# Whole chunks instead of half chunks behind the two norms of a 256-token sequence

## The chip, the cores and the metric

One NeuronCore of a Trainium2 chip runs the whole program in one launch. The metric is device time in microseconds, from the first to the last instruction; lower is better. The program is a bidirectional encoder layer over two sequences, one of 256 tokens and one of 512.

## What is computed

The reference, cut to what matters here:

```python
def encoder_layer(x, ...):
    h = rmsnorm(x, norm1_g)
    proj = h @ w_in                                  # 1024 -> 3584 columns
    ...                                              # attention heads, retention heads
    x = x + jnp.concatenate([na_o, ret_o], axis=-1) @ w_out
    x = x + peer(rmsnorm(x, norm2_g), peer_w_q, peer_sub_keys, peer_u, peer_v)
    return x

def peer(h, w_q, sub_keys, u, v):
    q = (ht @ w_q)...                                # 1024 -> 2048 columns
    ...                                              # top keys, experts, gelu(h @ u), @ v
```

`reference()` applies this to `x_prompt` (256 tokens) and `x_sample` (512 tokens), then a last norm.

## The kernel before

All five engines run hand-written programs that are ordered by semaphores. The sequence index is `q`: 0 for the 256 tokens (`TILES[0] = 2` tiles of 128 tokens) and 1 for the 512 tokens (4 tiles). The order of stages is `front(0)`, 128 expert steps for `q = 0`, `front(1)`, 128 expert steps for `q = 1`, then the sum over expert rows and the last norm.

`front(q)` reads 52 weight chunks of 512 KB in a fixed order (`C_NA_QK` 0 to 7, `C_NA_V` 8 to 11, and so on, up to `C_WQ` 36 to 51). Each chunk goes through a ring of `RING = 4` slots: SyncE loads it to `raw` once the chunk four places ahead has been split, ScalarE copies it to the rounded high part `sp_hi` (line 536) when its slot has been read, and VectorE makes the low part `sp_lo = raw - sp_hi` (line 1145). The normalised tokens are held in the same way, as `ht_hi` and `ht_lo`. A product in full precision is then three matmuls: high by high, low by high, high by low. All these are matmuls of type fp32r.

Behind a norm, VectorE scales a token tile into `h_tile` (line 1170), TensorE turns it by 8 transposes (`turn`, line 845), ScalarE writes `ht_hi` out of PSUM (line 570), and VectorE writes `ht_lo` (`turned_lo`, line 1181, counted by the semaphore `lo_evac`). This is done tile by tile.

A channel-major chunk is 8 x 3 = 24 matmuls that add up in one PSUM bank. `t_part` (line 863) runs them over all tokens of the sequence: 256 columns for `q = 0`, 512 for `q = 1`. `t_half` (line 879) runs them over half of the tokens: 128 columns for `q = 0`, 256 for `q = 1`. `first_chunks` runs the first two chunks behind a norm in halves, so that the first halves can start when half of the tiles have been turned. It is called for chunks 0 and 1 of the 256-token sequence, for chunks `C_WQ` and `C_WQ + 1` of both sequences, and nowhere else. The chunks that follow are run whole. `front(0)` has 8 channel-major chunks behind the first norm, then token-major ones with 512 columns (line 833), and 16 behind the second norm, then `key_scores` (line 1052).

VectorE's program between the first norm and the fourth chunk holds `log_decays`, a chain of small operations; its `lo(0, 3)` stands after it.

Of the kernel before, what the change touches and what calls it, by code (L numbers as in the profile page):

```python
# [79 lines left out]
def encoder_program(nc, a):  # L80
# [3 lines left out]
    with ctx:  # L84
# [159 lines left out]
        def counted(q, name, n):  # L244

            return S[name], (first_counts[name] if q else 0) + n

        def tile_cols(t):
            return slice(t * P, (t + 1) * P)
# [4 lines left out]
        def slot_of(q, c):  # L254
            return c % RING
# [4 lines left out]
        def t_index(c):  # L260

            return c if c < C_NA_V else c - 4 if c < C_RET_V else c - 20
# [566 lines left out]
        def _(pe):  # L829
# [7 lines left out]
            def turn(q, n, i):  # L837

                tt = n * TILES[q] + i
                pe.wait_ge(*counted(q, "src_ready", tt + 1))  # L840
                if i >= 2:
                    pe.wait_ge(*counted(q, "lo_evac", tt - 1))
                bank = 2 + 2 * (tt % 2)
                for k in range(KD):
                    last = pe.transpose(ps[:, bank + k // 4, tile_cols(k % 4)], h_tile[:, i % 2, tile_cols(k)],
                                        s["ident"][:, :])
                last.then_inc(S["tr_done"], 1)

            def t_part(q, c, first, end):

                n, w = t_index(c), TILES[q] * P
                sl = slot_of(q, c)
                if first == 0:
                    pe.wait_ge(*counted(q, "lo_ready", c + 1))
                    if n >= 2:
                        pe.wait_ge(*counted(q, "t_evac", n - 1))
                    elif q:
                        pe.wait_ge(S["gelu_done"], N_KEYS - 1 + n)
                for e in range(first, end):
                    k, which = e // 3, e % 3  # L860
                    lhs = (sp_hi, sp_hi, sp_lo)[which][:, sl, k * P:(k + 1) * P]
                    x = (ht_hi, ht_lo, ht_hi)[which][q][:, k, :]
                    last = pe.matmul(ps[:, n % 2, 0:w], lhs, x, start=e == 0, stop=e == 23, skip_group_check=True)  # L863
                if end == 24:
                    last.then_inc(S["t_done"], 1)

            def t_half(q, c, m):

                n, w = t_index(c), TILES[q] * P // 2
                sl, cols = slot_of(q, c), slice(m * w, m * w + w)  # L870
                if m == 0:
                    pe.wait_ge(*counted(q, "lo_ready", c + 1))
                    if n >= 2:
                        pe.wait_ge(*counted(q, "t_evac", n - 1))
                for e in range(24):
                    k, which = e // 3, e % 3
                    lhs = (sp_hi, sp_hi, sp_lo)[which][:, sl, k * P:(k + 1) * P]
                    x = (ht_hi, ht_lo, ht_hi)[which][q][:, k, cols]
                    last = pe.matmul(ps[:, n % 2, cols], lhs, x, start=e == 0, stop=e == 23, skip_group_check=True)  # L879
                if m == 1:  # L880
                    last.then_inc(S["t_done"], 1)

            def first_chunks(q, n, c):

                nt = TILES[q]
                for i in range(nt - 1):
                    turn(q, n, i)
                if nt == 2:
                    turn(q, n, 1)
                pe.wait_ge(*counted(q, "lo_evac", n * nt + nt // 2))  # L890
                t_half(q, c, 0)
                if nt > 2:
                    turn(q, n, nt - 1)
                t_half(q, c + 1, 0)
                pe.wait_ge(*counted(q, "lo_evac", n * nt + nt))
                t_half(q, c, 1)
                t_half(q, c + 1, 1)
# [18 lines left out]
            def front(q):  # L916
# [3 lines left out]
                if q == 0:  # L920
                    first_chunks(0, 0, C_NA_QK)
                else:
                    pe.wait_ge(*counted(q, "lo_evac", nt))
# [101 lines left out]
                for c in range(C_OUT + 2, C_WQ):  # L1025
                    if c == C_OUT + 4:
                        pe.wait_ge(*counted(q, "v_evac", 3 * nt))
                    v_chunk(q, c)
                first_chunks(q, 2, C_WQ)
                for c in range(C_WQ + 2, C_END):  # L1030
                    t_chunk(q, c)
# [797 lines left out]
```

## Time and profile before

| what | value |
|---|---|
| runs | 2477.81, 2489.20, 2477.03 us; median 2477.81 |
| profiled execution, first to last instruction | 2478.5 us |
| mean granted TensorE clock | 0.979 |
| TensorE busy | 2372.6 us (96%) |
| VectorE busy | 1798.1 us (73%) |
| GpSimd busy | 1276.9 us (52%) |
| ScalarE busy | 1057.5 us (43%) |

The profile has no other time of its execution than the span. A share of busy time is a mean over stages with different limits. The granted clock is given as a share of 2.4 GHz: 0.50 is 1.2 GHz and 1.00 is 2.4 GHz.

### The profile page before, as it was taken

Reading aid. Unit: us, or ns where it says so; the run is one execution under the profiler, and the core shown is the slowest. Engines: PE = TensorE matmul, PEld = TensorE weight load, DVE = VectorE, ACT = ScalarE, POOL = GpSimd, SP = SyncE. Lnnn points to the kernel's source line nnn. Section 1 sums busy time; section 2 is a strip of 40 time slices with the busy share of each in tenths; the row PEclk is TensorE's granted clock in tenths of the full one; section 3 lists DMA queues with packets and bytes.
Section 4 is the critical chain, followed back from the end, with each engine's and each line's share of the span. In section 5 each row is a group of like instructions: output and inputs, shape, how many; then the busy total and the mean of one; then the engine's idle time right before and its main releaser. Section 6 shows DMA issues by size and latency. Waiting matters only on the chain.

```text
span 2478.5 us, 34835 instructions
## 1 busy us (share of the span) xinstructions
PE 2372.6 (96%) x12777; PEld 2025.7 (82%) x12777; DVE 1798.1 (73%) x3382; ACT 1057.5 (43%) x1810; POOL 1276.9 (52%) x892
## 2 busy tenths in 40 slices
PE   7988999999999998999999999999999999999997
PEld 7768999999977766787787788788788788888886
DVE  4673696454367797659999778477587688888886
ACT  4443454554334322332333276366474333333333
POOL 0000599000352355547777756287374488888860
PEclk9987999999999999999999999999999999999999
DMA  4533677767764447556576678978988999999994
GB/s 160 162 128 100 221 223 220 262 216 231 245 195 133 158 143 260 197 193 193 179 221 196 193 237 282 319 244 292 337 288 277 329 336 357 340 349 349 346 365 159
DMA packets 252681, 596.86 MB, mean 241 GB/s; under 512 B 35792, under 2 KB 118224, under 8 KB 251872
## 3 DMA queue, kind: packets, MB, share of 16 engines
q1 hardware_dynamic: 182496, 385.69, 46.4%
q0 software_dynamic: 67712, 201.61, 25.0%
q10 hardware_dynamic: 2304, 7.34, 1.0%
q8 instruction: 102, 1.67, 0.3%
q14 instruction: 67, 0.55, 0.1%
HBM read 521.12 MB, written 73.40 MB: 240 GB/s over the span
## 4 chain that ended last, share of the span: by engine, by line
PE 35%; POOL 16%; DVE 5%; issue 4%; DMA 4%; ACT 2%; SPq 1%; DVEq 0%; ACTq 0%
PE ps L833 27%; POOL a_got L479 8%; POOL picked L474 7%; PE ps L863 3%; PE ps L1081 3%; DMA raw<-in_experts 2%; POOL sp_lo L470 1%; DMA picked<-in_experts,vidx 1%; DVE acc_odd L1568 1%; DVE acc L1568 1%; ACT sp_hi L697 1%; PE ps L879 0%; SPq L359 0%; DVE sp_lo L1617 0%; DMA v_raw<-in_experts 0%
## 5 line engine op out<-in xcount | busy, mean ns | idle before, releaser
L474 POOL DMA_INDIRECT picked<-in_experts,vidx x384 | 484.2, 1261 | 659.4 <-PE ps L833 219.6
L833 PE MATMUL ps<-ht_hi,sp_hi 128*128 128x256 f32 (+1 forms) x2048 | 703.0, 343 | 17.6 <-POOL sp_lo L470 14.4
L833 PE MATMUL ps<-ht_lo,sp_hi 128*128 128x256 f32 (+1 forms) x2048 | 691.8, 338 | 0.0
L833 PE MATMUL ps<-ht_hi,sp_lo 128*128 128x256 f32 (+1 forms) x2048 | 691.4, 338 | 0.0
L479 POOL DMA_INDIRECT a_got<-acts,aidx x384 | 485.7, 1265 | 121.7 <-issue 108.0
L470 POOL TENSOR_TENSOR sp_lo<-raw,sp_hi 128x1024 fp32r<-128x1024 f32 x112 | 303.7, 2726 | 358.8 <-ACT sp_hi L697 358.4
L833 PEld LDWEIGHTS ps<-ht_hi,sp_hi 128*128 128x128 f32 x2048 | 391.1, 191 | 60.7 <-POOL sp_lo L470 18.9
L833 PEld LDWEIGHTS ps<-ht_hi,sp_lo 128*128 128x128 f32 x2048 | 390.6, 191 | 41.4
L833 PEld LDWEIGHTS ps<-ht_lo,sp_hi 128*128 128x128 f32 x2048 | 391.3, 191 | 36.6
L1617 DVE TENSOR_TENSOR sp_lo<-raw,sp_hi 128x1024 fp32r<-128x1024 f32 x144 | 176.4, 1225 | 265.4 <-ACT sp_hi L697 265.0
L705 ACT ACTIVATE act_g<-ps 128x256 f32<-128x256 f32 (+1 forms) x256 | 125.8, 491 | 546.3 <-PE ps L833 546.0
L833 PE MATMUL ps<-v_hi,w_hi 128*128 128x512 f32 x768 | 301.3, 392 | 9.1 <-DVE v_lo L1608 4.8
L833 PE MATMUL ps<-v_hi,w_lo 128*128 128x512 f32 x768 | 299.7, 390 | 0.0
L833 PE MATMUL ps<-v_lo,w_hi 128*128 128x512 f32 x768 | 299.6, 390 | 0.0
L697 ACT ACTIVATE sp_hi<-raw 128x1024 fp32r<-128x1024 f32 x256 | 269.3, 1054 | 45.2 <-DMA raw<-in_experts 45.0
L734 ACT ACTIVATE v_hi<-v_raw 128x1024 fp32r<-128x1024 f32 x128 | 135.8, 1061 | 338.7 <-PE ps L833 333.8
L1568 DVE SCALAR_TENSOR_TENSOR acc<-picked,wts,acc 128x1024 f32<-128x1024 f32 x192 | 253.8, 1322 | 19.7 <-DMA picked<-in_experts,vidx 19.6
L1568 DVE SCALAR_TENSOR_TENSOR acc_odd<-picked,wts,acc_odd 128x1024 f32<-128x1024 f32 x189 | 251.8, 1332 | 15.2 <-DMA picked<-in_experts,vidx 14.9
L1145 DVE TENSOR_TENSOR sp_lo<-raw,sp_hi 128x1024 fp32r<-128x1024 f32 x104 | 126.9, 1223 | 151.4 <-ACT sp_hi L536 136.7
L1608 DVE TENSOR_TENSOR v_lo<-v_raw,v_hi 128x1024 fp32r<-128x1024 f32 x128 | 156.6, 1224 | 74.5 <-ACT v_hi L734 74.3
L833 PEld LDWEIGHTS ps<-v_hi,w_hi 128*128 128x128 f32 x768 | 144.5, 188 | 47.4 <-issue 9.1
L833 PEld LDWEIGHTS ps<-v_hi,w_lo 128*128 128x128 f32 x768 | 144.5, 188 | 30.4
(190 smaller groups left out, 3659.9 us busy)
## 6 DMA issues: line engine op xcount, KB each, us to landing
raw<-in_experts SPq DMA_DIRECT2D x256, 512.0 KB, 4.2
v_raw<-in_experts SPq DMA_DIRECT2D x128, 512.0 KB, 6.0
raw<-in_front SPq DMA_DIRECT2D x104, 512.0 KB, 3.8
acts<-act_g SPq DMA_DIRECT2D x128, 256.0 KB, 4.5
act_in<-acts SPq DMA_DIRECT2D x128, 192.0 KB, 6.0
acts<-act_g SPq DMA_DIRECT2D x128, 128.0 KB, 2.3
gates<-stage SPq DMA_DIRECT2D x16, 1024.0 KB, 8.9
g_in<-gates SPq DMA_DIRECT2D x128, 128.0 KB, 6.1
```

The source lines that it names most:

```text
L470: pool.tensor_tensor(sp_lo[:, k], raw[:, k], sp_hi[:, k].bitcast(F32), ALU.subtract).then_inc(S["u_lo"], 1)
L474: pool.indirect_dma_start(picked[n % SLOTS][:, :], None, v_rows, bass.IndirectOffsetOnAxis(ap=vidx[:, n // P, n % P:n % P + 1], axis=0)).t ...
L479: pool.indirect_dma_start(a_got[:, n // P, n % P:n % P + 1], None, acts[n // P // 2], bass.IndirectOffsetOnAxis(ap=aidx[:, n // P, n % P:n ...
L697: act.activation(sp_hi[:, k], raw[:, k], ACT.Copy).then_inc(S["u_hi"], 1)
L705: act.activation(act_g[q][:, step % 2], ps[:, step % 2, 0:TILES[q] * P], ACT.Gelu_apprx_tanh).then_inc(S["gelu_done"], 1)
L734: act.activation(v_hi[r % 3][:, :], v_raw[r % RING][:, :], ACT.Copy).then_inc(S["v_hi"], 1)
L833: last = pe.matmul(out, l, r, start=start and k == 0, stop=stop and k == 2, skip_group_check=True)
L863: last = pe.matmul(ps[:, n % 2, 0:w], lhs, x, start=e == 0, stop=e == 23, skip_group_check=True)
L1145: dve.tensor_tensor(sp_lo[:, k], raw[:, k], sp_hi[:, k].bitcast(F32), ALU.subtract).then_inc(S["lo_ready"], 1)
L1568: last = dve.scalar_tensor_tensor(o[:, :], row, w, o[:, :], ALU.mult, ALU.add)
L1608: dve.tensor_tensor(v_lo[r % 3][:, :], v_raw[r % RING][:, :], v_hi[r % 3][:, :].bitcast(F32), ALU.subtract).then_inc(S["v_lo"], 1)
L1617: dve.tensor_tensor(sp_lo[:, k], raw[:, k], sp_hi[:, k].bitcast(F32), ALU.subtract).then_inc(S["u_lo_dve"], 1)
```

## The change

For a sequence of two tiles, both tiles are turned, TensorE waits for the low parts of both, and the first two chunks run whole, over 256 columns, by `t_part`. For the sequence of four tiles nothing is changed in what runs.

```diff
--- before.py
+++ after.py
@@ -887,10 +887,13 @@
                     turn(q, n, i)
                 if nt == 2:
                     turn(q, n, 1)
+                    pe.wait_ge(*counted(q, "lo_evac", n * nt + nt))
+                    t_part(q, c, 0, 24)
+                    t_part(q, c + 1, 0, 24)
+                    return
                 pe.wait_ge(*counted(q, "lo_evac", n * nt + nt // 2))
                 t_half(q, c, 0)
-                if nt > 2:
-                    turn(q, n, nt - 1)
+                turn(q, n, nt - 1)
                 t_half(q, c + 1, 0)
                 pe.wait_ge(*counted(q, "lo_evac", n * nt + nt))
                 t_half(q, c, 1)
```

## Rows read from the trace of the kernel before

**Rows 1.** The page: busy time of TensorE, and its clock in 40 slices.
```profile
PE 2372.6 (96%) x12777; PEld 2025.7 (82%) x12777; DVE 1798.1 (73%) x3382; ACT 1057.5 (43%) x1810; POOL 1276.9 (52%) x892
...
PEclk9987999999999999999999999999999999999999
```

**Rows 2.** The page: the chain that ended last, by engine.
```profile
PE 35%; POOL 16%; DVE 5%; issue 4%; DMA 4%; ACT 2%; SPq 1%; DVEq 0%; ACTq 0%
```

**Rows 3.** Timeline, 16 to 59 us: start, duration, engine, line, operation.
```profile
16.81 1.22 DVE L1145 TENSOR_TENSOR sp_lo<-raw,sp_hi 128x1024 fp32r<-128x1024 f32 x1
...
18.17 0.45 PE L879 MATMUL ps<-ht_hi,sp_hi 128*128 128x128 f32 x1 [1.32 <-DVE sp_lo L1145]
...
19.09 2.16 DVE L1181 SCALAR_TENSOR_TENSOR ht_lo<-ps,g,ht_hi 128x128 fp32r<-128x128 f32 x8 [1.07 <-ACT ht_hi L570]
...
38.68 0.52 PE L863 MATMUL ps<-ht_hi,sp_hi 128*128 128x256 f32 x1
...
43.61 0.28 PE L863 MATMUL ps<-ht_hi,sp_lo 128*128 128x256 f32 x1
...
58.11 0.40 PE L833 MATMUL ps<-sp_hi,ht_hi 128*128 128x512 f32 x1
```

**Rows 4.** Timeline, 200 to 267 us.
```profile
202.81 0.47 PE L879 MATMUL ps<-ht_hi,sp_hi 128*128 128x128 f32 x1
...
204.96 2.16 DVE L1181 SCALAR_TENSOR_TENSOR ht_lo<-ps,g,ht_hi 128x128 fp32r<-128x128 f32 x8 [2.20 <-ACT ht_hi L570]
...
223.35 0.52 PE L863 MATMUL ps<-ht_hi,sp_hi 128*128 128x256 f32 x1
...
227.89 0.28 PE L863 MATMUL ps<-ht_hi,sp_hi 128*128 128x256 f32 x1
...
265.56 0.28 PE L863 MATMUL ps<-ht_hi,sp_lo 128*128 128x256 f32 x1
```

**Rows 5.** Windows: stretch, length, busy of each engine, clock, DMA share, GB/s.
```profile
18.00:38.60 20.60, 20.43 (x96) 20.46 (x97) 11.81 (x45) 5.89 (x11) 0.00 (x0) 1.00 0.50 164
...
203.00:208.00 5.00, 5.00 (x25) 5.00 (x25) 3.04 (x9) 2.87 (x9) 0.00 (x0) 0.50 0.00 0
...
223.30:227.80 4.50, 4.50 (x23) 4.50 (x23) 1.23 (x1) 1.33 (x2) 0.00 (x0) 0.50 0.22 77
...
160.00:180.00 20.00, 15.50 (x60) 12.59 (x61) 12.26 (x33) 7.54 (x11) 0.00 (x0) 0.76 0.52 189
...
900.00:996.00 96.00, 80.86 (x392) 63.14 (x392) 78.26 (x144) 28.80 (x51) 43.70 (x40) 0.93 0.57 195
...
1950.00:2300.00 350.00, 347.83 (x1521) 283.88 (x1520) 297.34 (x440) 125.21 (x170) 277.06 (x184) 1.00 0.97 341
```

**Rows 6.** Line 879, whole trace: durations in ns (least, median, most).
```profile
L879 PEld LDWEIGHTS ps<-ht_hi,sp_hi x96: 186/333/333, 18.1 to 1014.2; 128*128 128x128 f32 x96
L879 PE MATMUL ps<-ht_hi,sp_hi x96: 278/415/579, 18.2 to 1014.3; 128*128 128x128 f32 x64, 128*128 128x256 f32 x32
```

**Rows 7.** Timeline, 512-column matmuls at the low clock, first and last of nine.
```profile
165.57 0.63 PE L833 MATMUL ps<-sp_lo,ht_hi 128*128 128x512 f32 x1
...
168.98 0.63 PE L833 MATMUL ps<-sp_hi,ht_hi 128*128 128x512 f32 x1
```

**Rows 8.** Timeline of the chunk ring, and from the page the loads' time to landing.
```profile
25.23 1.06 ACT L536 ACTIVATE sp_hi<-raw 128x1024 fp32r<-128x1024 f32 x1 [0.70 <-issue]
...
29.64 1.22 DVE L1145 TENSOR_TENSOR sp_lo<-raw,sp_hi 128x1024 fp32r<-128x1024 f32 x1
...
204.77 1.10 ACT L536 ACTIVATE sp_hi<-raw 128x1024 fp32r<-128x1024 f32 x1
...
raw<-in_front SPq DMA_DIRECT2D x104, 512.0 KB, 3.8
```

## The prediction

> **What bounds the kernel now.** I read the page first: TensorE is busy 2372.6 of 2478.5 us (96%), no other engine over 73% [rows 1]. Busy is not the same as at its peak, so I asked next for the chain that ended last: its largest entry is TensorE's own matmuls (35%), then GpSimd's gathers (16%) [rows 2]. Those gathers belong to the expert stages after the change. The change itself sits in the 256-token front end, so I went to the timeline of its two places and to the windows around them.
>
> *Place 1* (start of the program). The low part of the first weight chunk is ready at 16.81 + 1.22 = 18.03 us, and the first narrow matmul follows at 18.17. The first 256-column matmul starts at 38.68: 96 narrow matmuls took 20.51 us, or 0.2136 us from start to start. The low parts of the second token tile are ready at 19.09 + 2.16 = 21.25 [rows 3]. The wide chunks behind begin slowly and change pace at 43.61; the stage after them starts at 58.11 [rows 3].
>
> *Place 2* (behind the second norm) is the same picture: narrow matmuls from 202.81 to 223.35 (20.54 us), the second tile's low parts ready at 204.96 + 2.16 = 207.12, the pace changes at 227.89, the last wide matmul starts at 265.56 [rows 4].
>
> The windows tell the clock. It is granted at 0.50 (1.2 GHz) from 203 to 227.8 us, through all the narrow matmuls and the first wide ones [rows 5]. For place 1 the column says 1.00 [rows 5], but the start-to-start time of 0.213 us and the weight load of 333 ns are those of place 2 (median and maximum of all weight loads on that line are 333 [rows 6]), so I take the clock there to be 1.2 GHz too, whatever the column records. The reader is to see two things: TensorE has no gap in either place, yet it works at the low clock; and a narrow matmul gives half the columns of a wide one.
>
> **The price of a narrow and of a wide matmul.** Before 227.89 the wide ones come in (227.89 - 223.35) / 21 = 0.216 us, the first step of 0.32 included; without it, 0.213. So at the low level a 128-column matmul costs the same 0.213 us as a 256-column one. Columns do set the price above that width: the 512-column ones at the low level come at (168.98 - 165.57) / 8 = 0.426 us [rows 7], twice that of 256. Below it something else does, and each matmul has its own weight load of 333 ns at that clock [rows 6]. At the high level a wide one costs (265.56 - 227.89) / 314 = 0.120 us [rows 4].
>
> The Trainium skill, page "TensorE: Matmul & The Clock Gate", section on the back-to-back issue gap, speaks against this change: it lets the gap go as columns divided by 1.2 GHz when the clock is low, so a 128-column matmul would cost half of a 256-column one. By it the change would save no matmul time at all and only add the wait. The trace disagrees: 0.213 us for both widths.
>
> **The change part by part**, each place for itself.
>
> 1. *Matmuls removed.* Two chunks in halves are 4 x 24 = 96 matmuls; whole they are 48. Forty-eight fewer at 0.2133 us is -10.24 us in each place, on TensorE's own path, since it has no idle time there.
>
> 2. *Later start.* All of it now waits for the second tile. The first matmul came 0.14 us after its releaser [rows 3], so it starts at 21.39 instead of 18.17 in place 1 (+3.22) and at 207.26 instead of 202.81 in place 2 (+4.45). Behind the wait on TensorE stands only the chunk work itself; the transposes are issued before it. ScalarE's and VectorE's work up to the second tile's low parts does not depend on these matmuls, so the releaser does not move.
>
> 3. *The clock.* In place 2 it rose 4.54 us after the first wide matmul (21 slow ones), in place 1 4.93 us after (23 slow ones), while 20.5 us of narrow ones never raised it [rows 3 to 5]. I take it that the wide ones do the same where they start earlier. Then place 1 has, from 21.39: 23 in 4.93 us, and the other 192 - 23 = 169 at 0.120 = 20.28, next stage at 46.60 instead of 58.11: **-11.5 us**. Place 2, from 207.26: 21 in 4.54 us, 384 - 21 = 363 at 0.120 = 43.56, end at 255.36 instead of 265.68: **-10.3 us**. So the clock is worth 4.5 us in each place beyond parts 1 and 2: the 48 wide matmuls that are new, and those that were slow before, are fast except the first 21 to 23.
>
> 4. *Supply of chunks.* Chunks are read every 2.88 us (24 x 0.120) sooner than now. In place 1 the fourth chunk's low part is the tight one: VectorE makes it only after the decay logarithms, at 29.64 + 1.22 = 30.86 [rows 8]. TensorE would want it at 21.39 + 4.93 + (72 - 23) x 0.120 = 32.2: 1.3 us to spare, priced at nothing. If the clock rose at once it would be wanted at 30.0 and cost 0.9. The chunks behind it need: high part after the slot is read (1.06 us), low part (1.22), and a load that was issued when the chunk four places ahead was split; a load lands 3.8 us after issue [rows 8] and four chunks are 11.5 us. The cover is 11.5 - 3.8 - 1.06 - 1.22 = 5.4 us; without it each chunk would be late by the excess. In place 2 the fourth chunk's high part is done at 204.77 + 1.10 [rows 8], long before it is wanted. No DMA, no other queue and no other engine's instruction is added or moved past another; SyncE's loads follow the low parts and shift with them.
>
> 5. *Passing on.* Everything behind is released by TensorE's chunks or their outputs, so I let the whole 21.8 us reach the end. What does not shift rigidly is where the clock falls and rises later: the windows 160 to 180 (0.76) and 900 to 996 (0.93) hold about 9.6 and 13.4 us at the low level [rows 5], which cost half of that, 11.5 us. I allow a quarter of it either way: 3 us.
>
> **Sum**: 2478.5 - 11.5 - 10.3 = 2456.7 for the profiled execution, whose span is 0.7 us above the median of the runs (2477.8); I predict 2456.0. Bounds of the one unseen term, the delay of the clock's rise: a microsecond of it costs 1 - 0.120/0.213 = 0.44 us. With no delay the gain is 21.8 + 0.44 x 9.5 = 26.0 (25.1 with the late fourth chunk); with twice the delay 17.6. That is 2452 to 2460, and with the 3 us of part 5, 2449 to 2463. A measurement here tells about 0.5% (12.4 us) from no change.
>
> **Rivals.**
> - *The clock stays low behind the pause.* If the wide matmuls that now follow an idle stretch kept 1.2 GHz to the end of both stages, place 1 would end at 21.39 + 192 x 0.2133 = 62.3 (+4.2) and place 2 at 207.26 + 384 x 0.2133 = 289.2 (+23.5): 2505.5, slower. For it: 20.5 us of unbroken narrow work did not raise the clock. Against: the wide ones raised it twice within 5 us. It decides from the point where the two delays sum to 26.0 / 0.44 = 59 us. Chance 0.03.
> - *A wide matmul costs as much as its two halves.* From 512 to 256 columns the price halves [rows 5, 7]; if it went on so, 48 wide matmuls would cost what 96 narrow ones do, nothing is saved in part 1, and the two waits remain: 2477.8 + 3.2 + 4.5 = 2485.5. Against it stands 0.213 us for both widths in one and the same stretch [rows 4]. Chance 0.02. (It is the page's rule on the gap, named above, that would have it so.)
> - *Only one place counts.* The gain of one is given back: in place 1 by the chunk ring (from loads that take over 3.8 + 5.4 = 9.2 us to land, while the band loads run beside them), or behind place 2 by the expert stages, where the DMA engines are 0.97 busy from 1950 to 2300 [rows 5] and would have to be tied to something other than the front end. Then 2466.3 or 2467.5, within 0.5%. Chance 0.10.
> - Forecast: 0.85.
>
> So faster by over 0.5%: 0.85; within it: 0.10; slower: 0.05. The range for 8 in 10 is 2449 to 2466: the likeliest case's own range, drawn up to the one-place case.
>
> **What the profile after should show.** First wide matmul of this function at 21.4, the 256-column pace changing from 0.213 to 0.120 us some 4.5 to 5 us later, the 512-column stage at about 46.6; 96 fewer matmuls; place 2 about 11.5 us earlier in everything, then with first matmul 4.45 us later against its transposes and a stage shorter by 10.3. The 25 us at 0.50 there (202.8 to 227.8) should shrink to about 9 (202.8 to 211.8 in the times of before), half of it idle. The prediction is wrong if the clock rises much later than 5 us after the wide start, if TensorE waits on a chunk's low part in place 1, or if the start of the 128 expert steps moved by about 22 us but the end did not.

## The result and the profile after

The changed kernel takes 2459.5 us (median of seven runs, 2454.5 to 2470.1) where the kernel before takes 2477.8 (2476.6 to 2489.2). The ratio is 0.9915 with a 95% interval of 0.9891 to 0.9939, so 21 us less (15 to 27). The ratio weighs all runs; the medians are 18.3 us apart, the means (2482.0 and 2461.2) 20.8. The forecast was 2456.0 us, range 2449 to 2466. The profiled execution spans 2454.3 us against 2478.5, at a mean granted clock of 0.982 against 0.979.

The page of the changed kernel, busy times, clock and chain, answers to [rows 1, 2]:

```profile
PE 2342.5 (95%) x12681; PEld 1997.8 (81%) x12681; DVE 1804.2 (74%) x3382; ACT 1057.2 (43%) x1810; POOL 1259.9 (51%) x892
...
PEclk9988999999999998999999999999999999999999
...
PE 40%; POOL 12%; DVE 6%; issue 3%; DMA 3%; ACT 2%; SPq 1%; DVEq 0%; ACTq 0%
```

12777 - 12681 = 96 matmuls are gone, and TensorE is busy 30.1 us less. The timeline of the two places of the changed kernel (start, duration, engine, line; the line numbers behind 890 are three higher) answers to [rows 3, 4]:

```profile
18.39 2.16 DVE L1184 SCALAR_TENSOR_TENSOR ht_lo<-ps,g,ht_hi 128x128 fp32r<-128x128 f32 x8 [1.07 <-ACT ht_hi L570]
...
20.60 0.58 PE L863 MATMUL ps<-ht_hi,sp_hi 128*128 128x256 f32 x1 [4.46 <-DVE ht_lo L1184]
...
26.10 0.28 PE L863 MATMUL ps<-ht_lo,sp_hi 128*128 128x256 f32 x1
...
46.12 0.40 PE L833 MATMUL ps<-sp_hi,ht_hi 128*128 128x512 f32 x1
...
194.30 2.16 DVE L1184 SCALAR_TENSOR_TENSOR ht_lo<-ps,g,ht_hi 128x128 fp32r<-128x128 f32 x8 [2.20 <-ACT ht_hi L570]
...
196.51 0.58 PE L863 MATMUL ps<-ht_hi,sp_hi 128*128 128x256 f32 x1 [4.46 <-DVE ht_lo L1184]
...
200.25 0.28 PE L863 MATMUL ps<-ht_hi,sp_lo 128*128 128x256 f32 x1
...
244.15 0.28 PE L863 MATMUL ps<-ht_hi,sp_lo 128*128 128x256 f32 x1
```

Read each place from the row of VectorE: it ends at 20.55 and 196.46, and the first wide matmul follows 0.05 us later. The bracket names what TensorE sat idle for: 4.46 us until the second tile's low parts. The wide matmuls then come slowly for 5.50 us in place 1 and 3.74 us in place 2. In place 1 the pace alone tells the level: the trace's first entry of the granted clock is the rise to 1.00 at 26.07 us (43.49 us in the trace of before), and the windows read 1.00 ahead of it for want of an entry. The windows of place 2 (length, busy time of each engine, clock, DMA share, GB/s) show the clock on either side, as [rows 5] do for before:

```profile
190.00:196.50 6.50, 1.97 (x8) 1.57 (x8) 4.30 (x18) 3.12 (x9) 0.00 (x0) 0.50 0.00 0
196.50:200.20 3.70, 3.69 (x17) 3.69 (x18) 1.09 (x1) 0.00 (x0) 0.00 (x0) 0.51 0.38 142
200.20:244.00 43.80, 43.80 (x367) 43.80 (x367) 14.70 (x12) 17.12 (x27) 0.00 (x0) 1.00 0.55 193
```

Where the 24.2 us between the two profiles came from can be followed by the starts of matching instructions:

| point | before | after | shift |
|---|---|---|---|
| second tile's low parts begin, place 1 | 19.09 | 18.39 | -0.7 |
| first 512-column matmul behind place 1 | 58.11 | 46.12 | -12.0 |
| second tile's low parts begin, place 2 | 204.96 | 194.30 | -10.7 |
| last 256-column matmul behind place 2 | 265.56 | 244.15 | -21.4 |
| first expert step of the second sequence written | 1111.72 | 1090.86 | -20.9 |
| end of span | 2478.5 | 2454.3 | -24.2 |

The first 0.7 us is the start of the program, which the change does not touch. Place 1 gave 11.3 and place 2 gave 10.7. Between them 1.3 us were lost, between place 2 and 1111 us another 0.5, and after 1111 us 3.3 were gained. The last of these is taken up in the last experiments, the 1.3 us in the part on the prediction.

The two places can also be timed by themselves in every profile, from the end of the second tile's low parts to the start of the next stage (line 833 behind place 1, line 1052 of before behind place 2). Place 1 takes 35.8 to 36.9 us in five profiles with halves and 24.5 to 25.6 in five with whole chunks; place 2 takes 58.4 to 59.2 in three and 48.4 to 49.4 in five. (Kernels with spare matmuls, other waits or more halves in a place are left out there.) Each place keeps its time whatever the other one does.

### The profile page after: what moved, and what is told of

Its sections match the earlier page's. It is cut to its first block, busy times and chain, and to the rows that moved or that the text cites. A ratio compares the mean times of both kernels' runs of the same rounds, so it can differ in the third digit from the quotient of the medians.

```text
span 2454.3 us, 34643 instructions
## 1 busy us (share of the span) xinstructions
PE 2342.5 (95%) x12681; PEld 1997.8 (81%) x12681; DVE 1804.2 (74%) x3382; ACT 1057.2 (43%) x1810; POOL 1259.9 (51%) x892
## 4 chain that ended last, share of the span: by engine, by line
PE 40%; POOL 12%; DVE 6%; issue 3%; DMA 3%; ACT 2%; SPq 1%; DVEq 0%; ACTq 0%
PE ps L833 33%; POOL a_got L479 6%; POOL picked L474 5%; PE ps L1084 3%; PE ps L863 3%; DMA raw<-in_experts 2%; POOL sp_lo L470 1%; DVE acc_odd L1571 1%; DMA picked<-in_experts,vidx 1%; ACT sp_hi L697 1%; DVE acc L1571 0%; PE ps L879 0%; SPq L359 0%; DVE att L1350 0%; DVE sp_lo L1620 0%
## 5 line engine op out<-in xcount | busy, mean ns | idle before, releaser
L474 POOL DMA_INDIRECT picked<-in_experts,vidx x384 | 472.7, 1231 | 669.3 <-PE ps L833 220.7
L833 PE MATMUL ps<-ht_hi,sp_hi 128*128 128x256 f32 (+1 forms) x2048 | 702.1, 343 | 17.8 <-POOL sp_lo L470 13.7
L1571 DVE SCALAR_TENSOR_TENSOR acc<-picked,wts,acc 128x1024 f32<-128x1024 f32 x192 | 252.0, 1313 | 14.3 <-DMA picked<-in_experts,vidx 14.2
L863 PE MATMUL ps<-ht_hi,sp_hi 128*128 128x256 f32 (+1 forms) x496 | 172.3, 347 | 8.9 <-DVE ht_lo L1184 8.9
```

What stands on the lines that cost most here:

```text
L474: pool.indirect_dma_start(picked[n % SLOTS][:, :], None, v_rows, bass.IndirectOffsetOnAxis(ap=vidx[:, n // P, n % P:n % P + 1], axis=0)).t ...
L833: last = pe.matmul(out, l, r, start=start and k == 0, stop=stop and k == 2, skip_group_check=True)
L1571: last = dve.scalar_tensor_tensor(o[:, :], row, w, o[:, :], ALU.mult, ALU.add)
```

## The experiments

A ratio is to the kernel before, run in the same job. The point that I read in every trace is the first expert step of the second sequence (`act_g`, 128x512), at 1111.72 us before. It lies behind everything that the change touches, but 850 us behind place 2. Where it matters I give the first expert step of the first sequence too (`act_g`, 128x256, at 277.33 us before), which lies right behind place 2.

### One place at a time

Against the changed kernel; `n == 0` keeps place 1 whole, `n == 2` place 2, and the other place runs as before:

```diff
                 if nt == 2:
                     turn(q, n, 1)
+                if nt == 2 and n == 0:
                     pe.wait_ge(*counted(q, "lo_evac", n * nt + nt))
                     t_part(q, c, 0, 24)
                     t_part(q, c + 1, 0, 24)
                     return
```

> The two chunks are whole behind the first norm alone; behind the second norm they stay in halves. Theory (each place pays for itself: 48 matmuls fewer at 0.213 us, less the wait, plus the earlier rise of the clock): the 512-column stage starts 11.5 us earlier and so do the expert steps, the second place keeps its 20.5 us of narrow matmuls at 0.50; the end is 10 to 12 us earlier, ratio about 0.995. Rival (only one place counts, and it is the second): the end stays within 3 us of before.

> The two chunks are whole behind the second norm alone. Theory: nothing moves up to 200 us, the stage behind ends about 10.3 us earlier (10 to 11), and the end follows by 10 to 12 us, ratio about 0.996. The sum of this gain and that of the first place alone gives the 21 us of the full change. Rival (only the first place counts): the expert steps start 10 us earlier and the end does not.

Measured: place 1 alone 0.9971 (0.9952 to 0.9990), place 2 alone 0.9984 (0.9965 to 1.0003). At the first expert step of the second sequence they are at 1100.06 and 1104.44, so 11.7 and 7.3 us early. Place 2 alone was 12.2 us early when the first sequence's expert steps began, but 2.2 of these it had already ahead of place 2, where nothing was changed; it lost part of its lead on the way. Neither rival holds at that point: both places count there. At the end the ratios say only 7 and 4 us, less than either place's share. So both were run again beside the whole change.

### The wait alone

```diff
-                pe.wait_ge(*counted(q, "lo_evac", n * nt + nt // 2))
+                pe.wait_ge(*counted(q, "lo_evac", n * nt + (nt if nt == 2 else nt // 2)))
                 t_half(q, c, 0)
```

> Before, with only the wait of the change: the narrow halves stay, but the first of them waits for the low parts of both tiles. Theory: each place starts later by 3.2 and 4.5 us, the narrow matmuls come every 0.213 us and never raise the clock, so the expert steps start 7.7 us later and the end is 6 to 9 us later, ratio about 1.003. Rival (the later start is what lets the clock rise, not the width): the clock rises within the narrow stretch and the loss is under 3 us or a gain.

Measured: 1.0023 (1.0000 to 1.0046), so 6 us slower (0 to 11); the first expert step of the second sequence is 7.8 us late. In place 2 of this kernel (windows as above):

```profile
209.20:229.70 20.50, 20.50 (x96) 20.50 (x97) 2.29 (x2) 1.33 (x2) 0.00 (x0) 0.50 0.14 42
229.70:232.20 2.50, 2.50 (x14) 2.50 (x14) 0.88 (x1) 1.33 (x2) 0.00 (x0) 0.50 0.20 80
232.30:240.00 7.70, 7.70 (x66) 7.70 (x65) 2.70 (x3) 2.91 (x5) 0.00 (x0) 1.00 0.44 138
```

All 96 narrow matmuls run at 0.50, though they start later. The clock rises 2.65 us after the first wide one. The later start does not raise the clock: the width does it. Its price is less clear than the 7.8 us look. Right behind place 2, at the first sequence's first expert step, this profile is only 5.6 us late. It started 0.6 us earlier, and its clock rose 1.5 and 1.8 us sooner behind the first wide matmul than in the profile of before, worth 1.5 us at 0.44 for each microsecond. With both put back it is 7.7 us late, as forecast.

### Twice as many halves

The third and fourth chunk behind the second norm are run in halves too:

```diff
                 t_half(q, c, 1)
                 t_half(q, c + 1, 1)
+                if nt == 2 and n:
+                    for d in (c + 2, c + 3):
+                        t_half(q, d, 0)
+                        t_half(q, d, 1)
...
-                for c in range(C_WQ + 2, C_END):
+                for c in range(C_WQ + (4 if q == 0 else 2), C_END):
                     t_chunk(q, c)
```

> Before, with four chunks in halves behind the second norm instead of two: 96 narrow matmuls more, 48 wide ones fewer. Theory (a narrow matmul costs 0.213 us at the low clock, and narrow ones do not raise it however many): 192 x 0.2133 = 41.0 us of narrow matmuls, then 21 slow wide ones, then 267 at 0.120; the stage ends 14.7 us later than before, ratio about 1.006. Rival (the clock rises after enough unbroken work of any width): it rises within the 41 us and the loss is well under 14 us.

Measured: 1.0089 (1.0056 to 1.0121), 22 us slower (14 to 30), and 14.1 us late at the first expert step of the second sequence. Its windows:

```profile
201.20:242.20 41.00, 41.00 (x192) 41.00 (x193) 6.96 (x12) 7.04 (x15) 0.00 (x0) 0.50 0.16 52
242.20:245.40 3.20, 3.20 (x17) 3.20 (x17) 1.22 (x1) 1.33 (x2) 0.00 (x0) 0.50 0.00 0
245.50:260.00 14.50, 14.50 (x124) 14.50 (x123) 5.27 (x5) 6.64 (x10) 0.00 (x0) 1.00 0.53 161
```

41.0 us without a gap, 192 narrow matmuls, and the clock does not leave 0.50. From the second tile's low parts to the next stage place 2 takes 73.4 us here and 59.2 before, so 14.2 us more, where 14.7 were forecast with 21 slow wide matmuls; there were 15. The profiled execution ends 26.7 us behind that of before, so 12.6 us were lost behind 1111 us, where nothing was changed. What lost them is open.

### What a narrow matmul costs at the high clock

The kernel before, with spare matmuls in front of the halves of place 2. They write to PSUM bank 7, which nothing reads at that time:

```diff
+            def fill(q, c, count):
+                pe.wait_ge(*counted(q, "lo_ready", c + 1))
+                sl = slot_of(q, c)
+                for k in range(count):
+                    pe.matmul(ps[:, 7, 0:2 * P], sp_hi[:, sl, 0:P], sp_hi[:, sl, 0:2 * P], start=True, stop=True,
+                              skip_group_check=True)
...
                     turn(q, n, 1)
+                    if n:
+                        fill(q, c, 36)
```

> Before, with 36 spare wide matmuls behind the transposes of the second place, so that the narrow halves begin at the high clock. It tells what a narrow matmul costs there and whether it keeps the clock. Theory (bound by its own weight load, which takes half the time at the high clock): 0.107 to 0.12 us each, and the clock holds or falls back after some microseconds; if it holds, the 96 take 11.5 us instead of 20.5 and the expert steps start about 4 us earlier than before in spite of 6.3 us of fillers. Rival (narrow ones cost 0.213 us at any clock): 20.5 us again, and the expert steps start 4 to 6 us later than before.

Measured: one run of 2477.4 us; 7.5 us early at the first expert step of the first sequence, where about 4 were forecast, and 6.0 at that of the second. Timeline, and the window over the 96 narrow matmuls:

```profile
207.10 0.22 PE L879 MATMUL ps<-ht_hi,sp_hi 128*128 128x128 f32 x1
...
217.65 0.28 PE L879 MATMUL ps<-ht_hi,sp_lo 128*128 128x128 f32 x1
217.77 0.33 PE L863 MATMUL ps<-ht_hi,sp_hi 128*128 128x256 f32 x1
```

```profile
207.10:217.70 10.60, 10.60 (x98) 10.60 (x96) 1.05 (x1) 1.33 (x2) 0.00 (x0) 1.00 0.14 49
```

(217.65 - 207.10) / 95 = 0.111 us, half of the 0.213 at the low clock and close to the 0.120 of a 256-column one. The clock stayed at 1.00 for the whole 10.6 us. Both levels agree: with 128 or with 256 columns a matmul of this kernel costs about the same. And narrow matmuls, which raised the clock in no profile, did not let it fall either in this one. Each has a weight load, which took 333 ns at the low clock [rows 6] and 192 here. These times are longer than the distance between two matmuls, so in the record the loads overlap, and their length is not the floor itself. That something in the weight load sets the floor fits the halving, but it is not shown: no run took the load away.

### Spare matmuls in the changed kernel's pauses

```diff
                 if nt == 2:
+                    if n:
+                        fill(q, c, 20)      # fill_both_gaps only
                     turn(q, n, 1)
+                    fill(q, c, 20 if n else 14)
                     pe.wait_ge(*counted(q, "lo_evac", n * nt + nt))
```

> The changed kernel with the spare wide matmuls only behind the second tile's transposes of each place (14 and 20). Theory: the clock rises 2.4 to 5.5 us after the first spare matmul, so with the second place's chunks 0 to 6 of their matmuls are still slow instead of 12 to 26; the expert steps start 2 to 3 us earlier than in the changed kernel. Rival: the same time as the changed kernel within 0.5 us.

> The changed kernel with spare wide matmuls into an unused PSUM bank where TensorE would idle: 14 behind the transposes of the first place, 20 before and 20 behind the second tile's transposes in the second. They add no result. Theory (wide matmuls raise the clock, a pause lets it fall): the chunks of the second place start at the high clock, the second tile's transposes there take 1.2 instead of 2.0 us, and those of the first place reach it 2 to 3 us earlier; the expert steps start 2.5 to 4 us earlier than in the changed kernel, ratio to before about 0.990. Rival (the fillers delay the chunks or change nothing about the clock): no earlier, or later by up to 1 us.

> The changed kernel with spare wide matmuls behind the second tile's transposes (14 and 20), timed. Theory: 2 to 5 us better than the changed kernel of the same job, by the clock alone; ratio to before 0.990 to 0.992. Rival: the 2452 us of its single run was luck, and it stands within 1 us of the changed kernel.

Measured. Behind the transposes only: 2452.0 us in its single run; timed, 0.9891 (0.9864 to 0.9917), median 2456.9, beside 0.9902 (0.9873 to 0.9931), median 2459.4, of the changed kernel in the same job. (One of its six runs took 6796.54 us; why is not known, and the ratio is of the other five.) In both gaps: 0.9925 (0.9904 to 0.9946) beside 0.9933 (0.9913 to 0.9953). The intervals overlap, so no gain over the changed kernel is shown at the end. The traces show what happened to the clock in place 2, first with the spare matmuls (fillers) behind the transposes, timed, then with both gaps filled:

```profile
189.40:194.10 4.70, 3.22 (x22) 3.02 (x20) 2.50 (x11) 3.12 (x9) 0.00 (x0) 0.86 0.00 0
194.20:200.00 5.80, 5.80 (x48) 5.80 (x49) 2.29 (x2) 1.33 (x2) 0.00 (x0) 1.00 0.27 93
```

```profile
188.50:193.20 4.70, 2.69 (x23) 2.49 (x21) 3.20 (x14) 3.12 (x9) 0.00 (x0) 1.00 0.00 0
194.10:197.30 3.20, 3.20 (x17) 3.20 (x16) 0.23 (x1) 0.00 (x0) 0.00 (x0) 0.50 0.50 164
197.50:200.00 2.50, 2.50 (x24) 2.50 (x23) 0.72 (x1) 1.33 (x2) 0.00 (x0) 1.00 0.03 7
```

With fillers behind the transposes, the clock rose during them and all 384 wide matmuls ran at the high clock: at the start of the first sequence's expert steps both of its profiles are 25.3 and 26.3 us ahead of before, where the changed kernel's three are 21.4 to 23.5 ahead. Against the changed kernel of the same job that is 3.1 us (single run) and 1.8 us (timed), about the 2 to 3 us of the theory. At the first expert step of the second sequence the two profiles part: the single run is 27.5 us ahead of before, 4.8 more than the changed kernel of its job, the timed one 23.5, where the changed kernel of its job was 24.4. With both gaps filled the second tile's transposes took 1.03 us instead of 1.97 (1.2 was forecast), and the clock held through the pause, but the fillers ran fast and left TensorE idle, and the clock fell just behind the start of the chunks; the 20 in the earlier gap gave nothing back. Its profile was ahead of the changed kernel's of the same job by 1.6 us at the first sequence's first expert step and by 0.9 at the second's, where 2.5 to 4 were forecast.

### The whole and its parts once more

> The changed kernel once more, to hold beside the fillers and beside the sum of the two places. Theory: the two gains at the start of the second sequence's expert steps (11.7 and 7.3 us in the profiles of the one-place kernels) add up, so that point is 19 to 22 us earlier and the end too, ratio 0.991 to 0.993. Rival (the gain of the first comparison was in part luck of the second half of the program): ratio 0.995 or above.

> The changed kernel beside the two one-place kernels on one chip. Theory (the gains of the places add): its gain at the end is the sum of theirs within the spread of the runs, 18 to 22 us, and at the first expert step of the second sequence it is 19 to 23 us early. Rival (each place alone is worth less because the gathers of the second half fall behind unless the start is 20 us earlier): it gains 5 us or more over the sum of the two.

> Whole chunks behind the first norm alone, a second time. Theory: 10 to 12 us at the first expert step of the second sequence, and as much at the end (ratio 0.995 to 0.996). Rival: 7 us at the end as the first time, with VectorE waiting on gathered rows for 40 us or more and the gathers on the chain that ended last from 1590 to 1800 us.

> Whole chunks behind the second norm alone, a second time. Theory: 7 to 11 us at the first expert step of the second sequence, and as much at the end (ratio 0.996 to 0.997). Rival: 4 us at the end as the first time, with the gathers on the chain from 1590 to 1800 us.

Measured, with the earlier runs beside them. "Early" is the shift of one profiled execution against before at 277.33 and at 1111.72 us, and "profile" its shift at the end of the span; "waits" is how long VectorE waited for gathered expert rows from 1100 to 2450 us in that profile (27.2 us before).

| kernel | ratio | gain at the end, us | early at 277 us | early at 1111 us | profile, us | waits, us |
|---|---|---|---|---|---|---|
| changed | 0.9915 (0.9891 to 0.9939) | 21.1 | 21.4 | 20.9 | 24.2 | 16.0 |
| changed, again | 0.9933 (0.9913 to 0.9953) | 16.6 | 23.2 | 22.7 | 22.3 | 19.0 |
| changed, third | 0.9902 (0.9873 to 0.9931) | 24.3 | 23.5 | 24.4 | 21.2 | 22.9 |
| place 1 | 0.9971 (0.9952 to 0.9990) | 7.2 | 14.0 | 11.7 | -0.9 | 49.1 |
| place 1, again | 0.9966 (0.9945 to 0.9986) | 8.4 | 10.4 | 12.3 | 6.9 | 31.9 |
| place 2 | 0.9984 (0.9965 to 1.0003) | 4.0 | 12.2 | 7.3 | 0.8 | 43.0 |
| place 2, again | 0.9966 (0.9946 to 0.9986) | 8.4 | 11.7 | 11.9 | 2.0 | 45.5 |

At 277 and 1111 us the parts add up: 26.2 and 22.1, then 19.0 and 24.2 for the two pairs, 20.9 to 24.4 for the whole. At the end they fall short: 11.2 and 16.8 against 16.6 to 24.3, with intervals of 5 to 7 us either way on each number. In the last job the whole gained 7.5 us more than the sum of its parts, which is the size that the rival named; but the three intervals together allow some 10 us either way (an estimate, their half-widths added as squares), so this decides nothing. The changed kernel once more (0.9933) fell just short of its forecast of 0.991 to 0.993, the third (24.3 us, and 24.4 at 1111 us) went past its 18 to 22 and 19 to 23, place 1 again missed its 0.995 to 0.996 by little and place 2 again met its 0.996 to 0.997, but neither passed all of its lead at 1111 us on to the end.

The traces point to the expert steps between 1650 and 1830 us (times of before). From 1650 to 1675 us the three changed profiles gain 6 us on before and the four one-place ones 1.6 to 3.6; from there to 1830 us the changed ones lose 0.7 to 2.1 of it and the one-place ones 4.6 to 9.7. Between 2000 and 2100 us all seven lose another 2 to 6. The chain of work from 1590 to 1800 us by line, for place 2 again and then for the changed kernel (third); the view breaks these lines off:

```profile
by line: POOL picked L474 24.0%; POOL a_got L479 23.9%; DMA raw<-in_experts 16.5%; PE ps L833 13.8%; issue 9.7%; DMA picked<-in_experts,vidx 3.4%; PE ps L1086 3.4%; DVE sp_lo L1622 2.9%; ACT sp_hi L697 1.5%; DVE acc_odd L1573 0.6%; DVE acc 
```

```profile
by line: PE ps L833 52.8%; PE ps L1084 17.5%; DMA raw<-in_experts 17.0%; SPq L359 2.8%; SPq L378 2.8%; ACT sp_hi L697 2.5%; DVE sp_lo L1620 2.4%; issue 1.0%; DVE hot_a L1537 0.5%; DVE hot_b L1531 0.3%; SPq L374 0.2%; SPq L365 0.2%; ACT act_
```

In one GpSimd's gathers set the pace, in the other TensorE does. The kernel before lies between: 32.3% for TensorE's line 833, 13.8% for the two gathers. The rival of this round, that the gathers keep up only if the start is 20 us earlier, does not hold as put: `halves_after_fill` was 6.0 us early at 1111 us and had TensorE on that chain for 50.8% and waits of 22.9 us. "Place 1, again" did not bear it out either: its waits are 31.9 us, not 40 or more, and its chain (33.4% and 15.8%) is like that of before. One profile is one execution, and executions of the kernel before spread over 2472.9 to 2493.4 us in these jobs. So it is shown where the one-place profiles lose their lead, and that gathers pace that stretch in three of the four. All six profiles with both places whole, with and without spare matmuls, have line 833 on that chain for 52.8 to 56.7%, and no one-place profile has it for over 33.4%. Chance alone would seldom sort them so; what decides it is open.

## Why the prediction was right

- **The matmuls removed.** Right: 96 fewer, and 0.213 us apiece at the low clock for either width. `waits_alone` and `more_halves` keep or add narrow ones and pay exactly that.
- **The later start.** Right: the first wide matmul came 0.05 us behind its releaser where 0.14 was put, 4.36 us later than the narrow one relative to the second tile's low parts in place 2 (196.51 - 194.30 against 202.81 - 204.96), against 4.45 forecast. `waits_alone` shows its price without the rest: 7.7 us, as forecast, once the clock and the start of the program are put back. That its 7.8 us at 1111 us agree without this is luck; right behind place 2 it read 5.6.
- **The clock.** The mechanism was right, its size was drawn from too few cases. I took the delays of before, 4.54 and 4.93 us; the changed kernel had 3.74 and 5.50. In all places without spare matmuls, in every profile, it lay between 2.4 (`more_halves`, place 1: 38.25 to 40.66) and 5.9 us (`place2_again`: 205.33 to 211.20). At 0.44 us for each microsecond that moves a place by 1.5 us at most, well inside the bounds that the range used, from no delay to twice the delay. The profile of before was at the slow end of its kind: behind halves the delay was 2.4 to 5.0 us in eleven cases, 3.5 in the mean, behind the pause 3.1 to 5.9 in ten, 4.5 in the mean. So the 11.5 and 10.3 us forecast from that one profile flatter the change a little; by the means of the stretches timed above place 1 is worth 11.2 us and place 2 10.1. The rival in which the clock stays low is refuted by every one of these profiles.
- **A wide matmul that costs its two halves**, the rule on columns: refuted at both levels, 0.213 against 0.213 us and 0.111 against 0.120. The gap that the Trainium skill gives in "TensorE: Matmul & The Clock Gate" (back-to-back issue gap), columns divided by 1.2 GHz at the low clock, does not hold for these fp32r matmuls with a weight load each. The prediction took it for more than it is: the same section calls it the gap of an isolated matmul and says that at few columns it counts too little, because it leaves out the weight load. So the page, read whole, did not speak against the change.
- **Supply.** Right: TensorE has no wait for a chunk's low part in place 1, and runs 167 matmuls from 26.10 to 46.01 without a gap.
- **Passing on.** Right in its result, not shown as a mechanism. The sum of the two places was 22.0 us against 21.8 forecast (11.3 + 10.7), a match that is closer than the spread of the clock's delays deserves. What moved the rest is what that part named and what it did not. The clock's own fall between the places goes with the 1.3 us lost there: the stretch at the low level is 6.8 us long (104.6 to 111.4, granted 0.50) where before had 3.4 (118.6 to 122.0, granted 0.50). The second profile with such a stretch of 6.8 us, `place1_again`, lost 1.3 us there too, and the one with 3.4 like before, `after_again`, lost nothing. The 3 us allowed for such things was too small for the end, though: from 1111 us to the end the three profiles of the changed kernel, one and the same program, take 1363.4, 1367.1 and 1370.0 us. And the assumption that what a stage gains reaches the end whole is not borne out by the one-place kernels, which passed on 4 to 8 us of 7 to 12. That it came true for the changed kernel, 16.6 to 24.3 us in three jobs around the forecast of 21.8, rests on something in the second half of the program that the prediction did not see; to that extent it was luck.
- **Only one place counts.** Refuted at 1111 us, where each place alone is early by 7 to 12 us. At the end each place alone gained 4 to 8 us, and the interval of the first run of place 2 just includes no gain.

## What to carry to other kernels

Before splitting a matmul to start earlier, look up from the trace what a matmul of half the width costs: here it cost the same, so halving doubled TensorE's time for these chunks in exchange for 3 to 4.5 us of earlier start. Look at the granted clock of the stretch as well: here a stream without a gap sat at 1.2 GHz for 41.0 us to its end, and what followed began at that clock. With run-to-run spreads as large as the gain, time the changed stretch itself, from what releases it to the next stage, in several profiles; a single shift at one later point carries the luck of the clock with it. Judge the end by repeated jobs.

## What was not expected of the hardware

- 192 narrow matmuls back to back, 41.0 us with TensorE busy throughout, left the clock at 0.50. Yet 96 of them kept it at 1.00 for 10.6 us once 36 wide ones had raised it.
- A 128-column fp32r matmul came every 0.213 us at the low clock and every 0.111 at the high one; a 256-column one 0.213 and 0.120.
- In the first 43 us the granted clock reads 1.00 though the matmuls keep the pace and the 333 ns weight loads of the low clock. The trace's first clock entry is the rise at 43.49 us; ahead of it the pace is the only reading.
- In `fill_both_gaps`, with 20 quick spare matmuls and then 2.06 us of idleness, the clock stayed at 1.00 over the pause and fell 0.7 us after dense wide work had begun again, for 3.4 us.
